# Strassen's seven block products for 18 of 22 column pairs in three feed-forwards, x resting in device memory meanwhile

## What is computed

```python
def modulate(x, g, shift, scale):
    return rmsnorm(x, g) * (1.0 + scale[:, None, :]) + shift[:, None, :]

def swiglu(h, w13, w2):
    gate, up = jnp.split(h @ w13, 2, axis=-1)
    return (jax.nn.silu(gate) * up) @ w2

cond = jax.nn.silu(c)
for i in range(DEPTH):
    ada = (cond @ ada_w[i] + ada_b[i]).reshape(-1, 3, 3, D_MODEL)
    h = modulate(x, norm_g[i, 0], ada[:, 0, 0], ada[:, 0, 1])
    x = x + 0.5 * ada[:, 0, 2, None, :] * swiglu(h, ffn_w13[i, 0], ffn_w2[i, 0])
    h = modulate(x, norm_g[i, 1], ada[:, 1, 0], ada[:, 1, 1])
    ...
    x = x + ada[:, 1, 2, None, :] * y
    h = modulate(x, norm_g[i, 2], ada[:, 2, 0], ada[:, 2, 1])
    x = x + 0.5 * ada[:, 2, 2, None, :] * swiglu(h, ffn_w13[i, 1], ffn_w2[i, 1])
return rmsnorm(x, final_g)
```

## Time and profile before

| | us |
|---|---|
| median of 3 runs | 1974.1 |
| lowest, highest | 1973.95, 1976.76 |
| the profiled execution, its own time | 1974.37 |
| its span | 1972.4 |
| PE busy | 1934.8 |
| DVE busy | 1071.1 |
| ACT busy | 657.1 |

### The profile page before, as it was taken

One profiled execution on the slowest core, in us unless ns is written; L12 is line 12 of the kernel. 1 busy time (PEld: TensorE's weight loads), 2 busy tenths in 40 slices (PEclk: granted clock), 3 DMA queues, 4 the chain that ended last, 5 costly groups with the idle time before them and its releaser, 6 DMA issues.

```text
span 1972.4 us, 25814 instructions
## 1 busy us (share of the span) xinstructions
PE 1934.8 (98%) x9352; PEld 1615.7 (82%) x9352; DVE 1071.1 (54%) x1588; ACT 657.1 (33%) x962; POOL 20.0 (1%) x21
## 2 busy tenths in 40 slices
PE   7899999999999999999999999999999999999998
PEld 5788888888779888888898888889877798888887
DVE  6755553385567655553365555537786763333333
ACT  6322222244234422232243232223444442223221
POOL 4000000000000000000000000000000000000000
PEclk9999999999999999999999999999999999999999
DMA  7665643234112556653336656332221223232332
GB/s 312 233 213 186 198 137 96 87 97 150 54 54 82 169 189 199 189 154 100 102 111 198 194 191 189 101 97 92 96 75 44 69 87 107 92 104 90 84 98 80
DMA packets 77045, 256.39 MB, mean 130 GB/s; under 512 B 8336, under 2 KB 10512, under 8 KB 76472
## 3 DMA queue, kind: packets, MB, share of 16 engines
q1 hardware_dynamic: 76784, 255.05, 40.8%
q10 hardware_dynamic: 200, 0.52, 0.1%
HBM read 253.43 MB, written 2.11 MB: 130 GB/s over the span
## 4 chain that ended last, share of the span: by engine, by line
PE 90%; DVE 5%; DMA 2%; issue 1%; ACT 1%; SPq 0%; DVEq 0%; ACTq 0%
PE acc L557 20%; PE acc L558 20%; PE acc L559 20%; PE outp L557 8%; PE outp L558 8%; PE outp L559 8%; DVE w_lo L1420 1%; PE outp L803 1%; ACT w_hi L1015 1%; DMA early_ada<-ada 1%; PE acc L899 1%; DMA raw<-w 1%; PE stat L559 1%; PE stat L557 1%; PE stat L558 1%
## 5 line engine op out<-in xcount | busy, mean ns | idle before, releaser
L557 PE MATMUL acc<-h_hi,w_hi 128*128 128x512 f32 (+1 forms) x1900 | 709.2, 373 | 12.1 <-DVE w_lo L1420 8.3
L558 PE MATMUL acc<-h_lo,w_hi 128*128 128x512 f32 (+1 forms) x1900 | 697.8, 367 | 0.0
L559 PE MATMUL acc<-h_hi,w_lo 128*128 128x512 f32 (+1 forms) x1900 | 697.5, 367 | 0.0
L1420 DVE TENSOR_TENSOR w_lo<-raw,w_hi 128x1024 fp32r<-128x1024 f32 (+2 forms) x365 | 409.1, 1122 | 474.7 <-ACT w_hi L1015 463.9
L1015 ACT ACTIVATE w_hi<-raw 128x1024 fp32r<-128x1024 f32 (+2 forms) x369 | 358.8, 973 | 380.2 <-PE outp L559 286.3
L557 PEld LDWEIGHTS acc<-h_hi,w_hi 128*128 128x128 f32 x1900 | 358.6, 189 | 81.6 <-DVE w_lo L1420 11.2
L558 PEld LDWEIGHTS acc<-h_lo,w_hi 128*128 128x128 f32 x1900 | 358.8, 189 | 59.9 <-issue 1.4
L559 PEld LDWEIGHTS acc<-h_hi,w_lo 128*128 128x128 f32 x1900 | 358.8, 189 | 58.8
L557 PE MATMUL outp<-g_hi,w_hi 128*128 128x512 f32 (+1 forms) x792 | 290.5, 367 | 0.0
L559 PE MATMUL outp<-g_hi,w_lo 128*128 128x512 f32 (+1 forms) x792 | 289.4, 365 | 0.0
L558 PE MATMUL outp<-g_lo,w_hi 128*128 128x512 f32 (+1 forms) x792 | 289.4, 365 | 0.0
(11 more groups left out here) (244 smaller groups left out, 1223.3 us busy)
## 6 DMA issues: line engine op xcount, KB each, us to landing
raw<-w SPq DMA_DIRECT2D x176, 512.0 KB, 3.4
ada_raw<-ada SPq DMA_DIRECT2D x128, 512.0 KB, 4.3
raw<-w SPq DMA_DIRECT2D x64, 384.0 KB, 3.1
raw<-w SPq DMA_DIRECT2D x64, 320.0 KB, 2.9
raw<-wa SPq DMA_DIRECT2D x33, 512.0 KB, 3.4
raw<-wb SPq DMA_DIRECT2D x32, 512.0 KB, 3.3
early_ada<-ada SPq DMA_DIRECT2D x8, 1024.0 KB, 17.5
x_tok<-x_rows SPq DMA_DIRECT2D x2, 1024.0 KB, 8.1
```

Of the source, the lines that this page charges most:

```text
L557: pe.matmul(bank, a_hi, b_hi, start=start, stop=False)
L558: pe.matmul(bank, a_hi, b_lo, start=False, stop=False)
L559: return pe.matmul(bank, a_lo, b_hi, start=False, stop=stop)
L1420: dve.tensor_tensor(w_lo[s][:, 0:n], raw[base % RAWS][:, 0:n], w_hi[s][:, 0:n].bitcast(F32), ALU.subtract).then_inc(lo_ready, 1)
```

## The change

In feed-forwards 1, 2 and 3 the first four pairs stay as they are (`PLAIN`). Each of the other 18 (`FAST`) is seen as a 2 by 2 block product: gate and up columns by two halves of the channels, times two halves of the channels by two halves of the tokens. Seven products of 4 row blocks by 256 tokens take the place of eight (in units of such blocks), 84 matmuls of 256 tokens in place of 48 of 512. The common sums of the token side (`right_sums`) are made once per feed-forward and split into `t_hi` and `t_lo`, which lie where `x`, `sq` and `ada_raw` were; `x` is stored to device memory as the modulated halves are made, and loaded back when the last pair is done. The sums of the weight side (`left_sum`) are made on DVE for each pair, in fp32, from two units, and split into seven 128 x 512 factors (three slots of two and one of one). Where a product is needed in more than one result, ACT copies the running sum from one PSUM place to another (`tap`, three for each pair) or to SBUF (`keep_shared`), while PE goes on; DVE adds the shared part to both halves of up before it multiplies. The pairs alternate between two sets of PSUM banks.

The `ada` tiles leave feed-forwards 1 and 2: eighty go into feed-forward 0, two with each unit, forty into the W2 stage of feed-forward 1, six with each output tile.

```diff
+PLAIN = 4
+FAST = FT - PLAIN
+FAST_SLOTS = 4
+UNITS_FAST = 2 * PLAIN + FAST_SLOTS * FAST + NW2
...
+        T1, T3, T2, T4 = range(4)
+        t_home = ((x_home + 8192, x_home + 12288), (sq_home, sq_home + 4096), (x_home, x_home + 4096),
+                  (ada_region, ada_region + 4096))
+        t_hi = [at(f"t_hi{i}", [P, KT // 2, H2], F32R, t_home[i][0]) for i in range(4)]
+        t_lo = [at(f"t_lo{i}", [P, KT // 2, H2], F32R, t_home[i][1]) for i in range(4)]
+        x_copy = nc.dram_tensor("x_copy", (P, KT, S), F32, kind="Internal").ap()
...
+        def right_sum(t):
+            rows, half = ((0, 0), (0, 1), (1, 1), (1, 0))[t]
+            return mod[:, rows * KT // 2:(rows + 1) * KT // 2, tok(half)]
...
+                sl = ADA_FIRST
+                step(0, 0, [(EARLY, k) for k in range(KT)], cuts=OPENING)
+                with sp.Fori(0, ADA_LOOP - 1) as i:
+                    step(1, 2 * i, [(sl, k) for k in range(KT)], 2 * i)
+                    step(2, 2 * i, [(sl + 1, k) for k in range(KT)], 2 * i)
+                i = ADA_LOOP - 1
+                step(1 + 2 * i, 0, [(sl + 2 * i, k) for k in range(KT)])
                 for m in range(4):
-                    load2(m, 0)
-                    for sl, k in before_w2[m:m + 1]:
-                        load_ada(sl, k)
+                    load2(0, m, 0)
+                    for s, k in tiles_of([(sl + 2 * i + 1, k) for k in range(KT)], m, EVEN):
+                        load_ada(s, k)
+                rest_of_w2(0)
...
+                def load_pair(j):
+                    for part, buffer in enumerate(fast_raw(j)):
+                        if j == 0:
+                            sp.wait_ge(lo_ready, B - RAWS + part + 1)
+                        elif j == 1:
+                            sp.wait_ge(t_lo_ready, 4 * (r + 1))
+                        else:
+                            sp.wait_ge(lo_ready, B + FAST_SLOTS * (j - 2) + 3)
+                        sp.dma_start(raw[buffer][:, :], w13[p * N13 + 2 * (PLAIN + j) + part])\
...
+                for i in range(4):
+                    load13(p, i)
+                store_x(0)
+                load13(p, 4)
+                load13(p, 5)
+                store_x(1)
+                load13(p, 6)
+                load13(p, 7)
+                for j in range(FAST):
+                    load_pair(j)
...
+                sp.wait_ge(unit_done, W)
+                sp.dma_start(x[:, :, :], x_copy).then_inc(x_loaded, 16)
...
+                for o in range(1, KT):
                     for m in range(4):
-                        load2(m, 1, o)
+                        load2(p, m, o)
+                        for sl, k in late_tiles(o - 1, m):
+                            load_ada(sl, k)
...
+                lows(0)
+                if j == 1:
+                    for k in range(4):
+                        pe.wait_ge(acc_free[k], T[k] + 2)
+                elif j:
+                    pe.wait_ge(gate_made, FAST * r + j - 1 + more)
+                    pe.wait_ge(product_made, FAST * r + j - 1 + more)
+                if j < 2:
+                    for bank in (gate[:, 0, 0:H2], up[:, 0, 0:H2]):
+                        pe.matmul(bank, w_hi[B % SLOTS][:, 0:P], h_hi[:, 0, 0:H2], start=True, stop=True)
+                term(gate[:, 1, 0:H2], 0, 0, *block_of_h(0, 0), True).then_inc(tap_ready, 1)
+                term(up[:, 1, 0:H2], 0, 1, *factor(T3, 2), True).then_inc(unit_done, 1)
+                lows(1)
+                pe.wait_ge(tap_done, first + 1)
+                term(gate[:, 1, 0:H2], 1, 1, *factor(T2, 3), False).then_inc(tap_ready, 1)
+                term(gate[:, 0, 0:H2], 1, 0, *block_of_h(1, 0), False).then_inc(unit_done, 1)
+                lows(2)
+                pe.wait_ge(tap_done, first + 2)
+                term(gate[:, 1, 0:H2], 2, 1, *factor(T1, 1), False).then_inc(tap_ready, 1)
+                term(up[:, 0, 0:H2], 2, 0, *factor(T4, 4), False).then_inc(unit_done, 1)
+                lows(3)
+                pe.wait_ge(tap_done, first + 3)
+                term(gate[:, 1, 0:H2], 3, 0, *block_of_h(1, 1), False).then_inc(unit_done, 1)
...
+                def tap(j, n):
+                    gate, up = fast_banks(j)
+                    dst = (gate[:, 0, 0:H2], up[:, 0, 0:H2], up[:, 1, H2:S])[n]
+                    act.wait_ge(tap_ready, 3 * (FAST * r + j) + n + 1)
+                    act.activation(dst, gate[:, 1, 0:H2], ACT.Copy).then_inc(tap_done, 1)
...
+                full_modulated()
+                for i in range(4):
+                    right_high(i)
+                gate_of(p, 2)
+                product_high(p, 2)
+                for n in range(3):
+                    factor_high(0, n)
+                for j in range(FAST):
+                    if j:
+                        fast_gate(j - 1)
+                    else:
+                        gate_of(p, 3)
+                    tap(j, 0)
+                    factor_high(j, 3)
+                    factor_high(j + 1, 0)
+                    tap(j, 1)
+                    if j:
+                        fast_high(j - 1)
+                    else:
+                        product_high(p, 3)
+                    factor_high(j + 1, 1)
+                    tap(j, 2)
+                    keep_shared(j)
+                    factor_high(j + 1, 2)
...
+                def right_sums():
+                    b11, b12, b22, b21 = (right_sum(t) for t in (T1, T3, T2, T4))
+                    dve.wait_ge(full_ready, KT * r + KT // 2)
+                    dve.tensor_tensor(b11, b11, b12, ALU.subtract).then_inc(t_summed, 1)
+                    dve.wait_ge(full_ready, KT * (r + 1))
+                    dve.wait_ge(t_summed, 4 * r + 1)
+                    dve.tensor_tensor(b12, b22, b12, ALU.subtract).then_inc(t_summed, 1)
+                    dve.wait_ge(t_summed, 4 * r + 2)
+                    dve.tensor_tensor(b22, b22, b11, ALU.add).then_inc(t_summed, 1)
+                    dve.wait_ge(t_summed, 4 * r + 3)
+                    dve.tensor_tensor(b21, b22, b21, ALU.subtract).then_inc(t_summed, 1)
...
+                def left_sum(j, n):
+                    if j == FAST:
+                        return
+                    gate, up = fast_raw(j)
+                    done = 3 * (FAST * r + j)
+                    if n == 0:
+                        for part, buffer in enumerate((gate, up)):
+                            count = loads(B + part) + j // 2 if buffer < RAWS else FAST_LOADS * r + j // 2 + 1
+                            dve.wait_ge(raw_loaded[buffer], 16 * count)
+                        if j:
+                            dve.wait_ge(lo_ready, B + FAST_SLOTS * (j - 1) + 3)
+                        else:
+                            dve.wait_ge(t_lo_ready, 4 * (r + 1))
+                        dve.tensor_tensor(arena[:, 8:10, :], arena[:, 2 * up + 1:2 * up + 3, :],
+                                          arena[:, 2 * up:2 * up + 1, :].broadcast_to([P, 2, 512]), ALU.add)\
+                           .then_inc(sums_ready, 1)
...
+                def fast_product(j):
+                    dve.wait_ge(unit_done, B + FAST_SLOTS * j + 3)
+                    dve.wait_ge(tap_done, 3 * (FAST * r + j + 1))
+                    dve.wait_ge(shared_kept, FAST * r + j + 1)
+                    up, y = up_halves(j), buf[j % 2][:, :].rearrange("p (a s) -> p a s", a=2)
+                    dve.tensor_tensor(up[:, 0:4:3, :], up[:, 0:4:3, :],
+                                      shared[j % 2][:, :].unsqueeze(1).broadcast_to([P, 2, H2]), ALU.add)\
+                       .then_inc(up_added, 1)
+                    dve.wait_ge(up_added, FAST * r + j + 1)
+                    dve.wait_ge(gate_made, FAST * r + j + 1)
+                    dve.scalar_tensor_tensor(out=y, in0=up[:, 0:4:3, :], scalar=-1.0, in1=y, op0=ALU.mult, op1=ALU.mult)\
+                       .then_inc(product_made, 1)
...
+                right_sums()
+                for i in range(4):
+                    right_low(i)
+                for n in range(3):
+                    left_sum(0, n)
+                product(p, 2)
+                product_low(p, 2)
+                factor_low(0, 0)
+                factor_low(0, 1)
+                for j in range(FAST):
+                    factor_low(j, 2)
+                    factor_low(j, 3)
+                    left_sum(j + 1, 0)
+                    if j:
+                        fast_product(j - 1)
+                    else:
+                        product(p, 3)
+                    left_sum(j + 1, 1)
+                    left_sum(j + 1, 2)
+                    if j:
+                        product_low(p, PLAIN + j - 1)
+                    else:
+                        product_low(p, 3)
+                    factor_low(j + 1, 0)
+                    factor_low(j + 1, 1)
...
+                if p:
+                    fast_pairs(p)
+                    dve.wait_ge(unit_done, W_FFN[p])
+                    dve.wait_ge(x_loaded, 16 * p)
...
```

(34 more changed lines are left out.)

378 lines of the change are left out of this document (271 added, 107 removed).

## The result

| | us |
|---|---|
| before, median of 4 runs | 1974.0 (1972.1 to 1976.8) |
| changed, median of 4 runs | 2003.1 (2001.8 to 2007.6) |
| ratio of the times, 95% interval | 1.015 (1.013 to 1.017) |
| profiled execution, its span | 2004.3, 2002.5 |

The change costs 29 us. The prediction was 1977, with 1950 to 1998 as its range: **wrong**. The mechanism of the loss and two of its three places stood in it, the whole at a third of its size.

A forecast was written before the change was run, and what follows sets the result against it. PE alone was taken to bound the kernel. 1974.4 - 29.7 (fast pairs) + 1.4 (spare matmuls) + 12.2 (transition waits) + 3.0 (clock) + 11 and 4 (`ada` tiles) + 0.5 (`x`) = 1976.8; forecast 1977 us, range 1950 to 1998.

The forecast's parts named there:

- What bounds the kernel: Whole kernel: PE alone sets the pace, busy 98% of the span; a fast pair takes 10.08 us against 10.88.
- Waits inside a fast pair: Fast pairs: PE's fifth product waits 0.25 us for the second tap, so a pair takes 10.33 us; 54 give 29.7.
- The chain of seven hops: Fast pair, first product's end to second tap over ACT and DVE: fifth product starts at 6.01 us, not 5.76.
- Plain to fast: Before the fast pairs of three feed-forwards: PE waits 5.4, 3.9 and 2.9 us, together 12.2, plus 3.0 for the clock.
- H: Start of the last early `w_hi` on ACT; the serial work before the fast pairs was counted to H + 20.6 us.
- `ada` tiles in feed-forward 0: Feed-forward 0, two tiles a unit: two units take 11.57 us for PE's 10.88, 11 us in all.
- Its reach: Feed-forward 0: 16 of the 20 loop rounds cost 0.69 us each, 11 us; 0 for its W2 stage.
- `ada` tiles in W2 of feed-forward 1: Six tiles for each output tile take 15.7 us for 14.96; PE waits 0.7 from the third on, 4 us in all.
- `x` coming back: After the last pair: reloading 2 MB takes 7.5 us, hidden behind the first output tile; 0.5 us late in feed-forward 2.
- Loads in feed-forward 0 fall further behind: Rival, chance 0.15: with three loads in flight landing goes to 5.0 us, two units take about 12.7; 1999.
- Loads that keep up: Rival, chance 0.30: fast pairs have no waits and tiles land in about 3.4 us; 1952.
- DVE becomes the bound: Rival, chance 0.08: in fast pairs, DVE operations costing 0.2 us more each bring the period to 10.9; 2006.

## Why the prediction was wrong, point by point

- **What bounds the kernel** (right). PE did, and a fast pair without waits takes 10.08 us, to the digit of the forecast (with the tap moved), from the pace of the earlier trace rows against that of the earlier trace rows.
- **Waits inside a fast pair** (right mechanism, size off). 10.33 was forecast, 10.235 measured. The chain of seven hops closed as walked and one swap opened it; it missed by 0.155 and not by 0.25, which gives 5 us more.
- **Plain to fast** (right). H + 20.6 was forecast and 20.61 measured in feed-forward 1. It is 20.61 and 20.60 in the other two. The waits were 5.05, 2.53 and 2.55 us for the forecast 5.4, 3.9 and 2.9, together 10.1 for 12.2. Half of the difference is H itself: in feed-forward 2 it stands 3.9 us behind the first matmul of 512 tokens (1070.75, 1066.87), and not 4.9 as in the kernel before. The clock fell behind all three, not two of them, and cost 2.4, 1.2 and 1.5 us, 5.1 for the forecast 3.0.
- **`ada` tiles in feed-forward 0** (the step that failed). The sum took "4.3 us until it lands" for each load and 11.57 for two units. Measured: 3.7 on the mean for the first of a burst and 5.1 for the second, with cycles of 12.24. In the cycle shown DVE starts the second tile at 294.95, the fourth at 301.33 and the second of the next cycle at 307.19: 6.38 us for the walked 5.7, and 5.86 for the walked 5.87. So the half with the silu work came out as walked, and the excess lies in the load behind the second tile, the one that DVE waits for. 4.3 was a median over loads in another company, one tile and one weight unit. Two units so cost 1.36 over PE's 10.88, not 0.69. The walk stood on the right rows and put landing at one number, where in these traces it went with how many were asked for together.
- **Its reach** (failed too). The excess was counted for 16 rounds and stopped at the end of the units. The last tiles come in the first W2 tile of feed-forward 0, where three waits of 2.39, 2.68 and 0.78 us and the clock behind the first made +8.4, costed at nothing.
- **`ada` tiles in W2 of feed-forward 1** (failed the same way). 15.7 was forecast for an output tile of 14.96; six residuals of the changed kernel stand 16.2 to 17.7 apart, 17.0 on the mean (927.98 to 1012.82). Between two of them the second tiles of the bursts start at 966.61, 972.14 and 978.42, and the next at 984.04: 5.5, 6.3 and 5.6 us, where 5.7, 4.9 and 5.1 were walked. The clock was costed at nothing here, and took 3.0 us behind waits of 2.08 and 3.34. +15.1, forecast 4.
- **`x` coming back** (right). 7.5 us was taken, 8.0 is the median of the three reloads; no PE wait came from one.
- **The rivals.** "Loads in feed-forward 0 fall further behind" (0.15) was the case: 5.0 us of landing and 12.7 for two units against 5.1 and 12.24. Its 1999 fell short because it had only 8 for W2 of feed-forward 1 (15.1) and nothing for W2 of feed-forward 0 (8.4). "Loads that keep up" (0.30) reasoned by bandwidth: 289 GB/s under 358 by the Trainium skill, "DMA: Bandwidth & Descriptors", section "Where 436 GB/s comes from". The trace agrees with that much, since 303 GB/s flowed with four buffers; but with two the kernel got 255. The queue had room, and the ring did not let it be used. "DVE becomes the bound" was not the case: DVE was busy 128 us of 150 with the tap moved, and that its 2006 lies nearest to 2003.1 is luck.

```profile
740.00:890.00 150.00, 150.00 (x1252) 150.00 (x1252) 127.65 (x150) 90.76 (x148) 0.00 (x0) 1.00 0.29 103
```
